# VectorE instead of GpSimd makes the low weight halves in the short convolution and first memory attention of a two-block float32 model

## The chip, the cores and the metric

The kernel runs as one program on one core of a Trainium2 chip. The core has a matrix engine (TensorE, PE in the rows), three engines for elementwise work (VectorE or DVE, ScalarE or ACT, GpSimd or POOL) and SyncE (SP), which here only issues loads. The metric is device time of one execution in microseconds, smaller being better.

## The reference, cut to what matters

The reference applies two blocks to 512 tokens of width 1024 in float32. The part that the change touches is the middle of the second block's first layer: a short gated convolution over 768 channels, and an attention of 512 queries over 256 memory tokens.

```
def short_conv_mixer(h, w_in, conv_w):
    proj = h @ w_in
    gate_b, gate_c, xt, q_mem = jnp.split(proj, [CONV_CH, 2 * CONV_CH, 3 * CONV_CH], axis=-1)
    y = gate_b * causal_short_conv(gate_c * xt, conv_w)
    return y, q_mem

def memory_attention(q_mem, mem, mem_norm_g, w_mem_kv, g_q, g_k):
    q = rms_norm(q_mem.reshape(b, s, MEM_HEADS, MEM_HEAD_DIM), g_q)
    k, v = jnp.split(rms_norm(mem, mem_norm_g) @ w_mem_kv, 2, axis=-1)
    k = rms_norm(k.reshape(b, m, MEM_HEADS, MEM_HEAD_DIM), g_k)
    ...
    p = jax.nn.softmax(scores, axis=-1).astype(v.dtype)
    o = jnp.einsum('bhqm,bmhd->bqhd', p, v)
...
        x = x + jnp.concatenate([y_mix, y_mem], axis=-1) @ w_out[layer]
```

## The kernel before, in words

Activations are kept transposed: channels on the 128 partitions, 512 tokens along the free dimension. Every weight matrix is cut into panels of 128x1024, each of which holds eight 128x128 blocks, and the panels are streamed from HBM in the order in which they are used (table `STAGES`, whose first number is the panels of a stage). One panel makes one 128x512 tile of output, in a bank of PSUM.

Each float32 product is made of three passes in a shorter type (fp32r). The weight panel is split into a high half `w_hi`, a rounded copy, and a low half `w_lo`, what the rounding left over; the activations have halves `h_hi` and `h_lo` likewise. A panel is then 8 x 3 matmuls: `w_hi*h_hi` (L640), `w_hi*h_lo` (L641) and `w_lo*h_hi` (L642).

A panel n passes four engines. SyncE loads it into one of four slots of `raw` once the low half of panel n-4 is made. ScalarE writes `w_hi` (L1259) into one of two slots, once TensorE has finished panel n-2. Then either VectorE (L1735) or GpSimd (L595) subtracts `w_hi` from `raw` into `w_lo`. TensorE waits for that low half, by one of the two counters `lo_ready` and `lo_by_pool`, and starts the panel.

Which engine makes the low half is read from the table `POOL_RUNS` (line 95): four runs of panel numbers belong to GpSimd, all others to VectorE. GpSimd has nothing else to do in a run but to wait for each `hi_ready` and subtract. VectorE's program is one fixed list of instructions written out by hand, in which a call `split(n)` stands at the place where panel n's low half is made, between the other work of the stage; `split` issues nothing for a panel of a GpSimd run. All engines work through their lists strictly in order.

The run named `conv` spans 23 panels, from the third panel of stage `conv0` to the first of `wo0`. The stages there are `conv0` (6 panels, two groups of three for the convolution), `qm0` (2, the queries of the memory attention), `conv1` (3), `mem0` (4, keys and values of 256 memory tokens, so that their matmuls are only 256 columns wide), `conv` (9, with the attention's steps between the panels) and `wo0` (8). I call the panels c0.0 to c0.5, q.0 and q.1, c1.0 to c1.2, m.0 to m.3, and c.0 to c.8.

VectorE's list there is, in short: for three panels of `conv0`, scale the tile by `rstd` (`scaled`, L1805), multiply, convolve (L1824, L1828), multiply, and make the halves of the result (L1740, L1741); then `memory_squares`, 16 instructions of 128x256 that sum the squares of the memory tokens; then the next three panels, the two of `qm0`, and `memory_input` for tiles 0 to 3 and, after the tile of c1.0, for tiles 4 to 7: three instructions of 128x256 each (L2370, L1740, L1741), which make the right-hand side of `mem0`. The lines that decide where a low half stands among these are:

```
                p = 3 * (j - head) + part
                if p or st is not ST["conv0"]:
                    split(st.n + p + 1)
...
            for j in range(4):
                split(ST["mem0"].n + j + 1)
```

Of the kernel before, what the change touches and what calls it, by code (L numbers as in the profile page):

```python
# [83 lines left out]
def schedule():  # L84
    out, n, t, s = {}, 0, 0, 0
    for name, panels, tiles, units in STAGES:
        out[name] = Stage(n, t, s, panels, tiles, units)
        n, t, s = n + panels, t + tiles, s + units
    return out, n


ST, PANELS = schedule()


POOL_RUNS = {"first": (ST["xbc"].n, ST["br0"].n),
             "conv": (ST["conv0"].n + 2, ST["wo0"].n), "s1a": (ST["s1a_in0"].n + 2, ST["s1a_in"].n - 1),
             "mla": (ST["mla_in"].n + 2, ST["wo1"].n)}


# [88 lines left out]
def at(c, i, step):  # L188

    return c if i is None else i * step + c  # L190
# [69 lines left out]
def build(nc, A, out):  # L260
    with ExitStack() as ctx:
# [292 lines left out]
        @block.sync  # L554
        def _(sp):
            wst = A["wstream"]
            sp.dma_start(vec[:, 0:DT], A["vec"][:, 0:DT]).then_inc(gain_loaded, 16)
            sp.dma_start(raw[:, 0], wst[0]).then_inc(w_loaded[0], 16)
            for k in range(DT):
                sp.dma_start(x[:, k], A["x"][:, k]).then_inc(x_loaded[k], 16)  # L560
            sp.dma_start(mats[:, 0:2], A["mats"][:, 0:2]).then_inc(ones_loaded, 16)
            sp.dma_start(raw[:, 1], wst[1]).then_inc(w_loaded[1], 16)
            sp.dma_start(mats[:, 2:], A["mats"][:, 2:]).then_inc(const_loaded, 16)
            sp.dma_start(vec[:, DT:], A["vec"][:, DT:]).then_inc(const_loaded, 16)
            for n in range(2, RAW):
                sp.dma_start(raw[:, n], wst[n]).then_inc(w_loaded[n], 16)

            def load(n, i=None):

                sp.wait_ge(lo_of(n), at(split_count(n), i, RAW))  # L570
                src = wst[n + RAW] if i is None else wst[bass.ds(i * RAW + (n + RAW), 1)].rearrange("a p n -> (a p) n")
                sp.dma_start(raw[:, n % RAW], src).then_inc(w_loaded[n % RAW], 16)

            for first, last in split_runs():
                last = min(last, PANELS - RAW - 1)
                rounds = (last - first + 1) // RAW
                if rounds > 1:
                    with sp.Fori(0, rounds) as i:
                        for n in range(first, first + RAW):
                            load(n, i)  # L580
                    first += rounds * RAW
                for n in range(first, last + 1):
                    load(n)


        @block.gpsimd
        def _(pool):
            def split_run(run):

                first, last = POOL_RUNS[run]  # L590
                whole = (last - first + 1) // RAW

                def one(n, i=None):
                    pool.wait_ge(hi_ready, at(n + 1, i, RAW))
                    nc.gpsimd.tensor_tensor(w_lo[:, n % HL], raw[:, n % RAW], w_hi[:, n % HL].bitcast(F32), ALU.subtract)\  # L595
                        .then_inc(lo_by_pool, 1)
                with pool.Fori(0, whole) as i:
                    for n in range(first, first + RAW):
                        one(n, i)
                for n in range(first + whole * RAW, last + 1):  # L600
                    one(n)

            split_run("first")
            pool.wait_ge(posted, ST["br0"].s + 8)
            pool.dma_start(rope_r[:], A["rope_r"]).then_inc(side_loaded, 16)
            pool.wait_ge(side_loaded, 16)
            pool.dma_start(tmp[:], A["ret_decay"]).then_inc(side_loaded, 16)
            pool.wait_ge(side_loaded, 32)
            for c in range(DT):
                pool.wait_ge(posted, ST["br2"].s + c + 1)  # L610
                k = c // 2 + RET_HEADS * (c % 2)
                pool.dma_start(x_in[:, k], A["x"][:, k]).then_inc(x_again[k], 16)
            pool.wait_ge(posted, ST["s0a_out"].s + 8)
            pool.dma_start(mem_x[:], A["mem"]).then_inc(side_loaded, 16)
            pool.wait_ge(side_loaded, 48)
            split_run("conv")
            split_run("s1a")
            pool.wait_ge(posted, ST["s1a_out"].s + 8)
            pool.dma_start(mem_x1[:], A["mem"]).then_inc(side_loaded, 16)
            pool.wait_ge(side_loaded, 64)  # L620
            pool.dma_start(rope2[:, 0].bitcast(I32), A["positions"].to_broadcast([P, S])).then_inc(side_loaded, 16)
            pool.wait_ge(side_loaded, 80)
            split_run("mla")
            last = ST["s1b_out"]
            for t in range(DT):
                pool.wait_ge(posted, last.s + t + 1)
                pool.dma_start(out[:, t], x[:, t]).then_inc(out_stored, 16)
            pool.wait_ge(out_stored, 16 * DT)
# [1091 lines left out]
        def _(dve):  # L1720
# [172 lines left out]
            def att_unit(a, u):  # L1893

                for first in range(a.ahead - 1) if u == 0 else ():
                    att_max(a, first)
                w = a.width(u)
                dve.wait_ge(a.exp_done, a.u0 + u + 1)
                done(v.reciprocal(small[:, a.columns(u, 2)], small[:, a.columns(u, 1)]))
                for e in range(a.chunks):  # L1900
                    prob = a.prob(u)[:, w * e:w * e + w]
                    ins = v.tensor_scalar(prob, prob, small[:, a.columns(u, 2, e)], None, ALU.mult)
                ins.then_inc(a.prob_ready, 1)
                if u + a.ahead - 1 < a.n:
                    att_max(a, u + a.ahead - 1)
                for hd in a.due(u, 1):
                    tile, _, last = a.tile(hd)
                    if last:
                        att_out(a, tile)
# [782 lines left out]
```

## Time and profile before

| | |
|---|---|
| time, median of 3 runs | 3110.13 us (3108.36 to 3115.47) |
| the profiled execution's own time | 3119.87 us |
| its span, first to last instruction | 3118.0 us |
| mean granted TensorE clock | 0.988 |
| TensorE busy | 3063.2 us, 98% |
| VectorE busy | 1822.0 us, 58% |
| ScalarE busy | 944.6 us, 30% |
| GpSimd busy | 247.1 us, 8% |

The span runs from the first to the last instruction, and the time of the execution is 1.87 us more. The stretch that the change concerns lies at about 1509 to 1680 us of the span. TensorE's clock is shown as a fraction of full speed; it has the two levels 2.4 and 1.2 GHz, so 0.50 is the lower one. In a timeline row the first number is the start in us, the second the duration in us, and the brackets at the end tell how long the engine had been idle and what released it.

### The profile page before, as it was taken

How to read it: one execution, taken by the hardware profiler on the slowest of the kernel's cores; microseconds unless marked ns; L12 is line 12 of the kernel's file. 1: busy time of each engine (PE TensorE's matmuls, PEld its weight loads, DVE VectorE, ACT ScalarE, POOL GpSimd, SP SyncE). 2: the span in 40 equal slices, each digit the busy share in tenths (PEclk: the TensorE clock that was granted, in tenths of full speed). 3: DMA queues.
4: the chain of work that ended last, by engine and by line, in shares of the span. 5: the costliest groups of instructions: out<-in, count | busy, mean ns of one | idle time of the engine just before them, and what ended most of it. 6: DMA issues, size and time to landing. Idle time of an engine off the chain costs nothing.

```text
span 3118.0 us, 36947 instructions
## 1 busy us (share of the span) xinstructions
PE 3063.2 (98%) x13711; PEld 2479.8 (80%) x13711; DVE 1822.0 (58%) x2429; ACT 944.6 (30%) x1294; POOL 247.1 (8%) x119
## 2 busy tenths in 40 slices
PE   8999999999999999999989999999999999999999
PEld 7787788787888878888777888887888886588887
DVE  8896565667666555554757554455554545565532
ACT  3644543333222222222222222222222243322222
POOL 0043330000000000000231000001000130000000
PEclk9999999999999999999999999999999997999999
DMA  4222133233223222223322223332233310023232
GB/s 143 95 94 81 62 101 115 68 108 102 94 95 100 96 92 92 98 94 108 108 81 75 95 94 101 102 101 88 97 98 103 110 62 27 22 96 98 94 108 88
DMA packets 79372, 287.60 MB, mean 92 GB/s; under 512 B 9056, under 2 KB 9312, under 8 KB 78880
## 3 DMA queue, kind: packets, MB, share of 16 engines
q1 hardware_dynamic: 77328, 277.96, 27.2%
q0 software_dynamic: 1936, 8.13, 0.8%
q8 instruction: 76, 1.25, 0.2%
q14 instruction: 32, 0.26, 0.0%
HBM read 283.96 MB, written 2.10 MB: 92 GB/s over the span
## 4 chain that ended last, share of the span: by engine, by line
PE 85%; issue 9%; DVE 3%; POOL 2%; ACT 1%; DMA 0%; POOLq 0%; DVEq 0%; ACTq 0%
PE ps L640 26%; PE ps L641 26%; PE ps L642 26%; POOL w_lo L595 2%; PE ps L733 1%; PE ps L1215 1%; PE ps L749 1%; PE ps L1076 1%; PE ps L1016 1%; PE ps L799 1%; PE ps L1221 1%; PE ps L1214 1%; PE ps L1082 0%; DVE w_lo L1735 0%; PE ps L698 0%
## 5 line engine op out<-in xcount | busy, mean ns | idle before, releaser
L1259 ACT ACTIVATE w_hi<-raw 128x1024 fp32r<-128x1024 f32 x525 | 555.5, 1058 | 1372.5 <-PE ps L642 1368.6
L640 PE MATMUL ps<-h_hi,w_hi 128*128 128x512 f32 (+1 forms) x2379 | 934.2, 393 | 6.8 <-DVE w_lo L1735 3.3
L641 PE MATMUL ps<-h_lo,w_hi 128*128 128x512 f32 (+1 forms) x2379 | 924.5, 389 | 0.0
L642 PE MATMUL ps<-h_hi,w_lo 128*128 128x512 f32 (+1 forms) x2379 | 924.2, 388 | 0.0
L1735 DVE TENSOR_TENSOR w_lo<-raw,w_hi 128x1024 fp32r<-128x1024 f32 x431 | 526.9, 1222 | 474.8 <-ACT w_hi L1259 469.8
L640 PEld LDWEIGHTS ps<-h_hi,w_hi 128*128 128x128 f32 x2379 | 448.2, 188 | 111.3 <-issue 11.2
L642 PEld LDWEIGHTS ps<-h_hi,w_lo 128*128 128x128 f32 x2379 | 447.9, 188 | 92.9
L641 PEld LDWEIGHTS ps<-h_lo,w_hi 128*128 128x128 f32 x2379 | 448.1, 188 | 92.1 <-issue 2.2
L640 PE MATMUL ps<-mid_hi,w_hi 128*128 128x512 f32 x1208 | 471.3, 390 | 2.2 <-DVE mid_lo L1810 2.1
L642 PE MATMUL ps<-mid_hi,w_lo 128*128 128x512 f32 x1208 | 470.7, 390 | 0.0
L641 PE MATMUL ps<-mid_lo,w_hi 128*128 128x512 f32 x1208 | 470.7, 390 | 0.0
L595 POOL TENSOR_TENSOR w_lo<-raw,w_hi 128x1024 fp32r<-128x1024 f32 x94 | 235.4, 2505 | 957.9 <-ACT w_hi L1259 949.9
L640 PEld LDWEIGHTS ps<-mid_hi,w_hi 128*128 128x128 f32 x1208 | 227.2, 188 | 51.1 <-DVE mid_lo L1810 3.5
L642 PEld LDWEIGHTS ps<-mid_hi,w_lo 128*128 128x128 f32 x1208 | 227.2, 188 | 47.4
L641 PEld LDWEIGHTS ps<-mid_lo,w_hi 128*128 128x128 f32 x1208 | 227.1, 188 | 47.2 <-issue 0.2
L1805 DVE TENSOR_TENSOR stage<-ps,rstd 128x512 f32<-128x512 f32 x104 | 71.8, 691 | 231.7 <-PE ps L642 231.6
L1264 ACT ACTIVATE stage<-ps 128x512 f32<-128x512 f32 x108 | 64.2, 599 | 372.3 <-PE ps L642 359.2
L640 PE MATMUL ps<-br_hi,w_hi 128*128 128x512 f32 x256 | 102.0, 398 | 11.2 <-DVE br_lo L1810 8.9
L1805 DVE TENSOR_TENSOR tmp<-ps,rstd 128x512 f32<-128x512 f32 x73 | 50.4, 691 | 99.8 <-PE ps L642 99.6
L642 PE MATMUL ps<-br_hi,w_lo 128*128 128x512 f32 x256 | 100.4, 392 | 0.0
L641 PE MATMUL ps<-br_lo,w_hi 128*128 128x512 f32 x256 | 100.4, 392 | 0.0
L1577 ACT ACTIVATE tmp<-tmp 128x512 f32<-128x512 f32 x112 | 69.3, 619 | 74.3 <-DVE tmp L1828 58.3
(402 smaller groups left out, 2616.8 us busy)
## 6 DMA issues: line engine op xcount, KB each, us to landing
raw<-in_wstream SPq DMA_DIRECT2D x525, 512.0 KB, 3.3
x<-in_x SPq DMA_DIRECT2D x8, 256.0 KB, 5.6
x_in<-in_x POOLq DMA_DIRECT2D x8, 256.0 KB, 3.1
mem_x<-in_mem POOLq DMA_DIRECT2D x2, 1024.0 KB, 5.1
out<-x POOLq DMA_DIRECT2D x8, 256.0 KB, 3.5
tmp<-in_ret_decay POOLq DMA_DIRECT2D x1, 1024.0 KB, 5.7
rope_r<-in_rope_r POOLq DMA_DIRECT2D x1, 512.0 KB, 4.0
mats<-in_mats SPq DMA_DIRECT2D x1, 256.0 KB, 6.5
```

What stands on the lines that cost most here:

```text
L595: nc.gpsimd.tensor_tensor(w_lo[:, n % HL], raw[:, n % RAW], w_hi[:, n % HL].bitcast(F32), ALU.subtract)\
L640: nc.tensor.matmul(dst, hi_w, hi_x, start=first, stop=False)
L641: nc.tensor.matmul(dst, hi_w, lo_x, start=False, stop=False)
L642: return nc.tensor.matmul(dst, lo_w, hi_x, start=False, stop=last)
L733: mm = nc.tensor.matmul(dst[:, n.heads * c:n.heads * c + n.heads], tmp[:, n.slots[j], P * c:P * c + P], ones, start=j == 0, stop=j == n.ti ...
L749: mm = nc.tensor.matmul(dst[rows, P * c:P * c + P], small[:, k:k + 1].to_broadcast([P, P // n.heads]), IDENT, start=True, stop=True)
L799: mm = nc.tensor.transpose(dst[:, o:o + P], a.prob(u)[:, w * e + P * c:w * e + P * c + P], IDENT)
L1259: nc.scalar.activation(w_hi[:, n % HL], raw[:, r], ACT.Copy).then_inc(hi_ready, 1)
L1264: nc.scalar.activation(dst, src[rows, 0:cols], func, bias=bias, scale=scale).then_inc(drained, 1)
L1577: nc.scalar.activation(tmp[:, s % 2], tmp[:, s % 2], func).then_inc(act_done, 1)
L1735: v.tensor_tensor(w_lo[:, n % HL], raw[:, n % RAW], w_hi[:, n % HL].bitcast(F32), ALU.subtract)\
L1805: v.tensor_tensor(dst, bank(t), scale, ALU.mult).then_inc(drained, 1)
```

## The change

The entry `conv` is taken out of `POOL_RUNS`, and the call that ran it out of GpSimd's program. The 23 panels then belong to VectorE by the same table, on all engines that ask it: `split` issues their low halves at the places where its calls already stand, TensorE and SyncE wait for `lo_ready` there, and GpSimd goes from its load of `mem_x` straight to waiting for the next run.

```
 POOL_RUNS = {"first": (ST["xbc"].n, ST["br0"].n),
-             "conv": (ST["conv0"].n + 2, ST["wo0"].n), "s1a": (ST["s1a_in0"].n + 2, ST["s1a_in"].n - 1),
+             "s1a": (ST["s1a_in0"].n + 2, ST["s1a_in"].n - 1),
              "mla": (ST["mla_in"].n + 2, ST["wo1"].n)}
...
             pool.dma_start(mem_x[:], A["mem"]).then_inc(side_loaded, 16)
             pool.wait_ge(side_loaded, 48)
-            split_run("conv")
             split_run("s1a")
```

The changed file has one line less, so VectorE's L1735 of before is L1734 of after, and so on.

First place: VectorE's list around `memory_squares`, between the third and the fourth panel of `conv0`. Before, from the end of the first convolution group:

```order
L1740 CAST cat_hi<-tmp 128x512
L1741 TENSOR_TENSOR cat_lo<-tmp,cat_hi 128x512
L1795 MEMSET acc 128x512
L1787 TENSOR_TENSOR stage<-mem_x 128x256
L1788 TENSOR_TENSOR acc<-acc,stage 128x256
...
L1805 TENSOR_TENSOR tmp<-ps,rstd 128x512
L1805 TENSOR_TENSOR stage<-ps,rstd 128x512
```

The same place in the changed program:

```order
L1739 CAST cat_hi<-tmp 128x512
L1740 TENSOR_TENSOR cat_lo<-tmp,cat_hi 128x512
L1794 MEMSET acc 128x512
L1786 TENSOR_TENSOR stage<-mem_x 128x256
L1787 TENSOR_TENSOR acc<-acc,stage 128x256
...
L1734 TENSOR_TENSOR w_lo<-raw,w_hi 128x1024
L1804 TENSOR_TENSOR tmp<-ps,rstd 128x512
L1734 TENSOR_TENSOR w_lo<-raw,w_hi 128x1024
L1804 TENSOR_TENSOR stage<-ps,rstd 128x512
```

The first `w_lo` is that of c0.4, the second that of c0.5. The one of c0.4 now stands behind the 17 instructions of `memory_squares`.

Second place: VectorE's list around `memory_input`, in stage `conv1`. Before, from the last of tiles 0 to 3 on:

```order
L1741 TENSOR_TENSOR mem_lo<-acc,mem_hi 128x256
L1805 TENSOR_TENSOR tmp<-ps,rstd 128x512
L2370 SCALAR_TENSOR_TENSOR acc<-mem_x,vec,spare 128x256
L1740 CAST mem_hi<-acc 128x256
...
L1741 TENSOR_TENSOR mem_lo<-acc,mem_hi 128x256
L1805 TENSOR_TENSOR stage<-ps,rstd 128x512
L2398 TENSOR_TENSOR cpad<-tmp,stage 128x512
```

The same place in the changed program:

```order
L1740 TENSOR_TENSOR mem_lo<-acc,mem_hi 128x256
L1734 TENSOR_TENSOR w_lo<-raw,w_hi 128x1024
L1804 TENSOR_TENSOR tmp<-ps,rstd 128x512
L2369 SCALAR_TENSOR_TENSOR acc<-mem_x,vec,spare 128x256
L1739 CAST mem_hi<-acc 128x256
...
L1740 TENSOR_TENSOR mem_lo<-acc,mem_hi 128x256
L1734 TENSOR_TENSOR w_lo<-raw,w_hi 128x1024
L1804 TENSOR_TENSOR stage<-ps,rstd 128x512
L2397 TENSOR_TENSOR cpad<-tmp,stage 128x512
```

The two `w_lo` are those of c1.1 and c1.2; each stands behind twelve instructions of `memory_input`.

Third place: VectorE's list at stage `mem0`. Before, from the end of the third convolution group:

```order
L1740 CAST cat_hi<-tmp 128x512
L1741 TENSOR_TENSOR cat_lo<-tmp,cat_hi 128x512
L1860 TENSOR_TENSOR tmp<-mem_k 128x256 x2
L1805 TENSOR_TENSOR tmp<-ps,rstd 128x512
L1868 RECIPROCAL small<-small 128x4 x2
```

The same place in the changed program:

```order
L1739 CAST cat_hi<-tmp 128x512
L1740 TENSOR_TENSOR cat_lo<-tmp,cat_hi 128x512
L1734 TENSOR_TENSOR w_lo<-raw,w_hi 128x1024 x4
L1859 TENSOR_TENSOR tmp<-mem_k 128x256 x2
L1734 TENSOR_TENSOR w_lo<-raw,w_hi 128x1024
L1804 TENSOR_TENSOR tmp<-ps,rstd 128x512
```

The four are the low halves of m.1, m.2, m.3 and c.0, one behind the other, and the single one is that of c.1.

## Rows read from the trace of the kernel before

**Rows 1.** The page: engines, and the two costliest groups that make low halves

```profile
PE 3063.2 (98%) x13711; PEld 2479.8 (80%) x13711; DVE 1822.0 (58%) x2429; ACT 944.6 (30%) x1294; POOL 247.1 (8%) x119
...
L1735 DVE TENSOR_TENSOR w_lo<-raw,w_hi 128x1024 fp32r<-128x1024 f32 x431 | 526.9, 1222 | 474.8 <-ACT w_hi L1259 469.8
...
L595 POOL TENSOR_TENSOR w_lo<-raw,w_hi 128x1024 fp32r<-128x1024 f32 x94 | 235.4, 2505 | 957.9 <-ACT w_hi L1259 949.9
```

**Rows 2.** Timeline of TensorE: starts of c0.2, c0.3, m.0 to m.3, c.0

```profile
1523.03 0.50 PE L640 MATMUL ps<-h_hi,w_hi 128*128 128x512 f32 x1
...
1528.60 0.39 PE L640 MATMUL ps<-h_hi,w_hi 128*128 128x512 f32 x1
...
1572.61 0.28 PE L640 MATMUL ps<-mem_hi,w_hi 128*128 128x256 f32 x1
...
1576.44 0.38 PE L640 MATMUL ps<-mem_hi,w_hi 128*128 128x256 f32 x1 [0.80 <-POOL w_lo L595]
...
1583.93 0.58 PE L640 MATMUL ps<-mem_hi,w_hi 128*128 128x256 f32 x1 [4.35 <-POOL w_lo L595]
...
1589.83 0.28 PE L640 MATMUL ps<-mem_hi,w_hi 128*128 128x256 f32 x1
...
1593.29 0.50 PE L640 MATMUL ps<-h_hi,w_hi 128*128 128x512 f32 x1 [0.80 <-POOL w_lo L595]
```

**Rows 3.** Windows of 4 us: length, PE busy (count), granted clock, DMA, GB/s

```profile
1580.00:1584.00 4.00, 0.07 (x1) 0.87 0.00 0
1584.00:1588.00 4.00, 4.00 (x19) 0.50 0.52 151
```

**Rows 4.** Timeline of TensorE in a later stage, around a shorter stall

```profile
2130.97 0.50 PE L640 MATMUL ps<-mid_hi,w_hi 128*128 128x512 f32 x1 [1.88 <-DVE mid_lo L1810]
...
2133.33 0.63 PE L640 MATMUL ps<-mid_hi,w_hi 128*128 128x512 f32 x1
...
2135.89 0.42 PE L640 MATMUL ps<-mid_hi,w_hi 128*128 128x512 f32 x1
```

**Rows 5.** Timeline of ScalarE: high halves after c0.3, q.1, c1.0; the drain of m.0

```profile
1534.30 1.06 ACT L1259 ACTIVATE w_hi<-raw 128x1024 fp32r<-128x1024 f32 x1 [4.38 <-PE ps L642]
...
1556.07 1.06 ACT L1259 ACTIVATE w_hi<-raw 128x1024 fp32r<-128x1024 f32 x1 [4.38 <-PE ps L642]
...
1561.99 1.06 ACT L1259 ACTIVATE w_hi<-raw 128x1024 fp32r<-128x1024 f32 x1 [4.50 <-PE ps L642]
...
1579.79 0.38 ACT L1264 ACTIVATE mem_k<-ps 128x256 f32<-128x256 f32 x1 [5.86 <-DVE stage L1805]
```

**Rows 6.** Timeline of GpSimd: the low half of c0.4

```profile
1530.00 2.54 POOL L595 TENSOR_TENSOR w_lo<-raw,w_hi 128x1024 fp32r<-128x1024 f32 x1 [3.40 <-ACT w_hi L1259]
```

**Rows 7.** Timeline of VectorE: first convolution group and the squares of the memory

```profile
1521.55 0.69 DVE L1805 TENSOR_TENSOR tmp<-ps,rstd 128x512 f32<-128x512 f32 x1
...
1528.87 0.69 DVE L1805 TENSOR_TENSOR stage<-ps,rstd 128x512 f32<-128x512 f32 x1 [0.42 <-PE ps L642]
...
1530.32 2.50 DVE L1740 CAST cat_hi<-tmp 128x512 fp32r<-128x512 f32 x1
...
1533.61 0.48 DVE L1795 MEMSET acc<- 128x512 f32 x1
...
1538.15 0.42 DVE L1787 TENSOR_TENSOR stage<-mem_x 128x256 f32<-128x256 f32 x1
...
1540.91 2.65 DVE L1787 TENSOR_TENSOR stage<-mem_x 128x256 f32<-128x256 f32 x1
```

**Rows 8.** Timeline of VectorE: the memory's reciprocal root and tiles 0 to 3

```profile
1557.52 1.75 DVE L2363 RECIPROCAL spare<-spare 128x256 f32<-128x256 f32 x1 [0.42 <-ACT spare L1319]
1559.31 0.58 DVE L2370 SCALAR_TENSOR_TENSOR acc<-mem_x,vec,spare 128x256 f32<-128x256 f32 x1
...
1562.97 0.48 DVE L2370 SCALAR_TENSOR_TENSOR acc<-mem_x,vec,spare 128x256 f32<-128x256 f32 x1
```

**Rows 9.** Timeline of VectorE in stage conv: one scaling

```profile
1635.18 0.69 DVE L1805 TENSOR_TENSOR stage<-ps,rstd 128x512 f32<-128x512 f32 x1 [4.47 <-PE ps L642]
```

More of the change, by code:

```diff
@@ L95 @@
 POOL_RUNS = {"first": (ST["xbc"].n, ST["br0"].n),
-             "conv": (ST["conv0"].n + 2, ST["wo0"].n), "s1a": (ST["s1a_in0"].n + 2, ST["s1a_in"].n - 1),
+             "s1a": (ST["s1a_in0"].n + 2, ST["s1a_in"].n - 1),
              "mla": (ST["mla_in"].n + 2, ST["wo1"].n)}
@@ L615, in _ @@
             pool.wait_ge(side_loaded, 48)
-            split_run("conv")
             split_run("s1a")
```

## The prediction

> **What bounds the kernel now.** I read the page first: TensorE is busy 98% of the span, VectorE 58%, GpSimd 8% [rows 1]. So the end is set by TensorE's panels and by the few places where TensorE waits, and a change that only reassigns elementwise work is worth what it adds to or takes from those waits. The same rows give the price of one low half: 1.22 us on VectorE (mean of 431), 2.5 us on GpSimd (mean of 94).
>
> Next I read TensorE's timeline through the stretch of the change. A panel of 512 columns takes 5.44 us: ScalarE's wait of 4.38 us plus its own 1.06 us repeat once a panel [rows 5]. One that follows a wait takes some 0.1 us more, as c0.2 does from 1523.03 to 1528.60 [rows 2]. TensorE loses nothing from there to m.0. Then it waits three times for GpSimd's low halves: 0.80 us before m.1, 4.35 us before m.2, 0.80 us before c.0 [rows 2]. The 4.35 us is followed by a stretch at a granted clock of 0.50, the 1.2 GHz level [rows 3], and m.2 takes 1589.83 - 1583.93 = 5.90 us [rows 2], against 8 x 3 matmuls in about 2.9 us for m.0 (3.83 us to the next start, less 0.80 idle and the slow restart).
>
> Last I asked why m.2 was late. ScalarE waited 5.86 us for VectorE's scaling of c1.2's tile before it could drain m.0 [rows 5]: that panel had ended at 1572.61, where m.0 starts, and VectorE came to it at 1579.06, the row's 1579.79 less 0.7 us for one scaling. VectorE was thus 6 us behind here. Until then its lateness had hurt nobody, since the low halves did not pass through it. That is the point of the argument: after the change they do.
>
> **A cost that goes.** In the rows of VectorE some instructions are 2 us too long: the cast at 1530.32 takes 2.50 us and ends with GpSimd's subtraction of 1530.00 to 1532.54 [rows 6, 7]; one square of 128x256 takes 2.65 us where its neighbour takes 0.42 [rows 7]. So nearly each of GpSimd's subtractions holds VectorE up for about 2.1 us. The Trainium skill (SBUF — State Buffer, Who interferes with whom) says that the two engines share a pair of ports under an exclusive lock, and that the second to come is blocked until the first ends; the trace agrees, with 2.50 us against 0.43. By that rule alone the move would shorten VectorE's work by about 2.1 - 1.2 = 0.9 us a panel, which speaks for a gain; it is the last of the rivals. I take the 2.1 us off wherever the trace shows one, from the rows and not from the rule.
>
> **The change, step by step.** I call the end of a panel 0.26 us before ScalarE's next high half (1534.30 for c0.3, whose end is then 1528.60 + 5.44 = 1534.04) [rows 2, 5].
>
> *A, c0.2.* GpSimd gave its low half for a start at 1523.03. VectorE now makes it behind the scaling of 1521.55 to 1522.24 [rows 7]: done at 1523.4, so +0.44 us.
>
> *B, c0.4.* c0.3 now ends at 1534.04 + 0.44 = 1534.5. VectorE goes on from the scaling of c0.2, 1528.87 + 0.44 = 1529.3. From there to the memset it took 4.74 us before, of which 2.07 was the held-up cast (2.50 against 0.43), so 2.67 us: the memset starts at 1532.0. Then 0.52 us for it, and 16 instructions at 0.46 (1538.15 to 1540.91 are six of them) [rows 7], 7.36 us: the low half starts at 1539.9, takes 1.22, and c0.4 starts at 1541.15. TensorE waits **+6.65 us** where it waited 0. Nothing hides it; behind it all of VectorE's and TensorE's list moves too. c0.5, q.0, q.1 and c1.0 do not wait again: VectorE has at most 5 us of work a panel there, of 5.44.
>
> *C, the clock behind B.* The nearest row is the 4.35 us wait, after which m.2 took 5.90 instead of about 3.0 us: **+2.9 us** [rows 2]. Bounds: 1.7 us (the shorter stall, below) and 3.4 us, twice that.
>
> *D, c1.1.* After the end of q.1 (1555.81), VectorE's reciprocal starts 1.71 us later, at 1557.52, and the first tile of `memory_input` 1.79 us after that; four tiles take 4.8 us (three took 3.66), then the low half 1.2: 9.5 us [rows 5, 8]. TensorE is done with c1.0 after 1561.99 - 1556.07 = 5.92 us [rows 5]. Stall **+3.6 us**.
>
> *E and F, the clock behind D, and c1.2.* In a later stage a wait of 1.88 us is followed by matmuls of 0.63 instead of 0.39 us, six of them in 2.56 us from 2133.33 to 2135.89, and nine or so in all: 1.7 us lost [rows 4]. I expect the same behind D. c1.2's low half stands behind a scaling, four tiles and itself, 0.66 + 4.8 + 1.2 = 6.65 us after that of c1.1, against a panel of 5.54: a wait of 1.1 us, which a slow c1.1 swallows. Together the larger: **+1.7 us** (bounds 1.1 and 2.9).
>
> *G, mem0.* From m.0's start to c.0's it took 1593.29 - 1572.61 = 20.7 us [rows 2]. Now VectorE is level with TensorE at the end of c1.2: 0.27 us to the scaling, 2.67 through the halves, 1.2 for the low half of m.1, so m.1 starts at 4.15 instead of at 2.9, a wait of 1.2. m.2 follows without one; m.3's high half comes 0.27 + 0.3 + 1.06 us after m.1's end at 7.0, its low half at 9.85, just when m.2 ends at 9.9; c.0 starts at 12.8. **-7.9 us**, from three waits made one and from 2.9 us of slow clock gone. Bounds: -8.8 if m.1 does not wait, -6 if m.2 and m.3 wait 1 us each.
>
> *The rest.* In `conv` the low half stands ahead of each scaling, that is before the panel's end that VectorE waits for anyway; in the attention units there it adds 1.2 us and the 2.1 us hold-ups go. 0, with bounds of -1 and +2. Loads start up to 6 us later behind B, and have three panels of slack: 0.
>
> Sum: 0.44 + 6.65 + 2.9 + 3.6 + 1.7 - 7.9 = **+7.4 us**. Against the profiled execution, 3118.0 us of span and 3119.87 us in all, that is 3125.4 and 3127.3; its time lies 9.7 us above the median of the runs, and I put the sum onto the median: 3110.1 + 7.4 = **3117.5 us**, +0.24%.
>
> **The rivals.** *Milder clock.* The stalls are as worked out, but the lower clock behind them is shorter or absent: B's at 1.7 and none behind D gives 0.44 + 6.65 + 1.7 + 3.6 + 1.1 - 7.9 = +5.6; no lower clock at all +3.9, so 3114 to 3115.7 us. For it: not every wait is followed by it (0.80 us before m.1 was not). Against: both stalls here are longer than the 1.88 us that was.
>
> *Later waits.* In the attention part VectorE is the engine that TensorE waits for, and a low half that queues behind a wait for ScalarE's exponentials or for a tile makes c.3 to c.8 late. At 1 to 2 us in three or four of six panels this gives +11 to +15, 3121 to 3125 us. Against: VectorE still has gaps there, 4.47 us before one of its scalings [rows 9].
>
> *The hold-ups were the real cost: faster.* If `memory_squares` and `memory_input` no longer delay a panel, because without GpSimd VectorE comes to them early enough, B to F vanish and -7.9 + 0.44 = -7.5 us is left, 3102.6 us. It decides at one point: VectorE would have to be at c0.4's low half by 1533.3, where I find 1539.9, and its 16 squares alone take 7.4 us of that stretch. I give it little.
>
> *No change in effect.* That B and G cancel: the backlog of VectorE is 6 us either way, and only its place moves, +2 to -2 us. For it: stalls of 0.44 + 6.65 + 3.6 + 1.1 + 1.2 against 5.95 before leave a difference that depends on the clock for half its size.
>
> **How the numbers follow.** My forecast, both stalls with a lower clock behind them (+5.8 to +9.5), 0.52; milder clock (+3.5 to +5.8) 0.23; later waits 0.10; no effect 0.09; faster 0.06. About 6.2 us, 0.2%, is what a measurement of this kernel can tell from no change, and it cuts my forecast's own range: 0.44 of its 0.52 lies above. So slower by over 0.2% is 0.44 + 0.10 = 0.54, within 0.2% 0.08 + 0.23 + 0.09 + 0.01 = 0.41, faster 0.05. The range goes from 3111.5, which leaves out the faster case and part of no effect, to 3122.5, which takes in the beginning of the later waits.
>
> **What would show it.** TensorE's waits in the new trace should name VectorE's low half: one of 6 to 7 us at about 1541, one of 3 to 4 us some 35 us later, one of about 1 us in `mem0`, and none for GpSimd in this stretch. Granted clock should be 0.50 just behind the first two and full in `mem0`. VectorE should show no cast or square over 1 us there. The prediction is wrong if c0.4 starts within 2 us of c0.3's end, if the waits come in `conv`, or if the slow stretch in `mem0` stays although its long wait is gone.

## The result, and the profile after

The changed kernel takes 3118.35 us (median of 20 runs, 3115.14 to 3126.64), the kernel before 3114.27 us (20 runs beside them, 3108.36 to 3118.77). The medians lie 4.1 us apart. The ratio of the two is given as 1.0019, with a 95% interval of 1.0013 to 1.0026, which is 5.9 us (4.0 to 8.1) slower. Forecast were 3117.5 us and +7.4 us.

The profiled execution of after took 3117.13 us, with a span of 3115.3 us. That is less than the 3118.0 us of the profiled execution before, although the medians go the other way. So two spans can't tell here what the change costs, and the stretch that it touches has to be cut out of the trace. I measure from VectorE's reciprocal at the head of `conv0` to its first low half in `wo0`. VectorE in the trace before, and in the trace after, where three of its rows in between stand too (start, duration, engine and line, operation, tiles, shapes):

```profile
1518.16 3.35 DVE L1799 RECIPROCAL rstd<-rstd 128x512 f32<-128x512 f32 x1 [1.94 <-ACT rstd L1299]
...
1678.93 1.23 DVE L1735 TENSOR_TENSOR w_lo<-raw,w_hi 128x1024 fp32r<-128x1024 f32 x1
```

```profile
1518.31 3.35 DVE L1798 RECIPROCAL rstd<-rstd 128x512 f32<-128x512 f32 x1 [1.94 <-ACT rstd L1298]
...
1530.84 0.43 DVE L1739 CAST cat_hi<-tmp 128x512 fp32r<-128x512 f32 x1
...
1539.91 1.23 DVE L1734 TENSOR_TENSOR w_lo<-raw,w_hi 128x1024 fp32r<-128x1024 f32 x1
...
1573.35 1.22 DVE L1734 TENSOR_TENSOR w_lo<-raw,w_hi 128x1024 fp32r<-128x1024 f32 x1
...
1684.94 1.23 DVE L1734 TENSOR_TENSOR w_lo<-raw,w_hi 128x1024 fp32r<-128x1024 f32 x1
```

The stretch is 1678.93 - 1518.16 = 160.77 us before and 1684.94 - 1518.31 = 166.63 us after: +5.86 us, which is what the ratio says (0.0019 x 3114.27 = 5.9). The rest of the span is 2957.2 us before and 2948.7 us after. Much of that difference arises in a later place that the change does not touch, and shows there in the granted clock (the number behind POOL's count). Two windows of 80 us from about the same point of the program, before and then after:

```profile
2465.00:2545.00 80.00, 76.87 (x385) 64.02 (x384) 36.31 (x55) 28.98 (x55) 23.17 (x11) 0.91 0.25 83
```

```profile
2471.00:2551.00 80.00, 76.99 (x419) 64.75 (x417) 40.62 (x59) 31.81 (x59) 25.20 (x12) 0.98 0.25 79
```

The stage was granted 0.91 in one execution, which started 385 matmuls in these 80 us, and 0.98 in the other, which started 419. One kernel alone varies as much from execution to execution: the 20 times of after go from 3115.14 us at a mean granted clock of 0.992 to 3126.64 us at 0.988. Over the kernels below the span outside the stretch goes from 2948.7 to 2959.7 us, and I take these 11 us for the same chance; that is inferred, since the one kernel that was profiled twice (after, and e8) repeated there within 0.7 us. It is more than the change itself.

The page of after, the lines that answer to [rows 1]:

```profile
PE 3054.4 (98%) x13711; PEld 2471.8 (79%) x13711; DVE 1816.4 (58%) x2452; ACT 944.8 (30%) x1294; POOL 189.9 (6%) x96
...
L1734 DVE TENSOR_TENSOR w_lo<-raw,w_hi 128x1024 fp32r<-128x1024 f32 x454 | 554.9, 1222 | 481.6 <-ACT w_hi L1258 475.9
...
L595 POOL TENSOR_TENSOR w_lo<-raw,w_hi 128x1024 fp32r<-128x1024 f32 x71 | 178.2, 2510 | 1016.1 <-ACT w_hi L1258 1012.9
```

23 low halves have changed engine (431 to 454, 94 to 71). VectorE's busy time is nevertheless 5.6 us shorter, since 23 x 1.22 = 28 us of new work is less than the hold-ups by GpSimd that went. (Within the stretch it falls from 114.5 to 109.1 us, so these were worth 33.5 us, 1.5 us for each of the 23 subtractions.) By the sum of busy time the change is thus a saving. What it costs is in when the work comes, which TensorE's waits of this stretch (total, times, longest) and its timeline show:

```profile
PE ps L639 <- DVE w_lo L1734: 12.0, 5, 6.4
```

```profile
1523.57 0.50 PE L639 MATMUL ps<-h_hi,w_hi 128*128 128x512 f32 x1 [0.54 <-DVE w_lo L1734]
...
1541.19 0.80 PE L639 MATMUL ps<-h_hi,w_hi 128*128 128x512 f32 x1 [6.40 <-DVE w_lo L1734]
...
1543.92 0.63 PE L639 MATMUL ps<-h_hi,w_hi 128*128 128x512 f32 x1
...
1546.04 0.40 PE L639 MATMUL ps<-h_hi,w_hi 128*128 128x512 f32 x1
...
1574.62 0.50 PE L639 MATMUL ps<-h_hi,w_hi 128*128 128x512 f32 x1 [3.43 <-DVE w_lo L1734]
...
1581.08 0.50 PE L639 MATMUL ps<-h_hi,w_hi 128*128 128x512 f32 x1 [0.69 <-DVE w_lo L1734]
...
1586.66 0.28 PE L639 MATMUL ps<-mem_hi,w_hi 128*128 128x256 f32 x1
...
1590.66 0.39 PE L639 MATMUL ps<-mem_hi,w_hi 128*128 128x256 f32 x1 [0.96 <-DVE w_lo L1734]
...
1599.44 0.40 PE L639 MATMUL ps<-h_hi,w_hi 128*128 128x512 f32 x1
```

Where GpSimd was waited for three times, 6.0 us in all, VectorE is now waited for five times, 12.0 us in all, in front of c0.2, c0.4, c1.1, c1.2 and m.1. Windows behind the three longest waits, and ScalarE, whose high half of a panel starts 0.26 us behind the end of an earlier one:

```profile
1540.00:1544.00 4.00, 2.81 (x7) 2.23 (x8) 2.87 (x3) 0.00 (x0) 0.00 (x0) 0.50 0.37 125
...
1572.00:1576.00 4.00, 1.38 (x6) 1.14 (x7) 3.86 (x9) 0.34 (x1) 0.00 (x0) 1.00 0.07 16
1588.00:1592.00 4.00, 3.04 (x26) 2.83 (x25) 3.38 (x5) 1.33 (x2) 0.00 (x0) 1.00 0.22 70
```

```profile
1534.89 1.06 ACT L1258 ACTIVATE w_hi<-raw 128x1024 fp32r<-128x1024 f32 x1 [4.38 <-PE ps L641]
...
1549.04 1.06 ACT L1258 ACTIVATE w_hi<-raw 128x1024 fp32r<-128x1024 f32 x1 [13.10 <-PE ps L641]
...
1571.29 1.06 ACT L1258 ACTIVATE w_hi<-raw 128x1024 fp32r<-128x1024 f32 x1 [4.50 <-PE ps L641]
```

Behind the 6.4 us wait the clock is 0.50, the 1.2 GHz level, and the matmuls take 0.63 us until about 1545; behind the 3.43 us wait it is 1.00, the 2.4 GHz level, against my forecast; in `mem0` it is full where [rows 3] had 0.50.

### The profile page after: what moved, and what is told of

It is laid out like the page before. It is cut to its first block, busy times and chain, and to the rows that moved or that the text cites. A ratio compares the mean times of both kernels' runs of the same rounds, so it can differ in the third digit from the quotient of the medians.

```text
span 3115.3 us, 36928 instructions
## 1 busy us (share of the span) xinstructions
PE 3054.4 (98%) x13711; PEld 2471.8 (79%) x13711; DVE 1816.4 (58%) x2452; ACT 944.8 (30%) x1294; POOL 189.9 (6%) x96
## 4 chain that ended last, share of the span: by engine, by line
PE 86%; issue 8%; DVE 4%; POOL 1%; ACT 1%; POOLq 0%; ACTq 0%; DVEq 0%
PE ps L639 26%; PE ps L641 26%; PE ps L640 26%; POOL w_lo L595 1%; PE ps L732 1%; PE ps L1075 1%; PE ps L1214 1%; PE ps L748 1%; PE ps L1015 1%; DVE w_lo L1734 1%; PE ps L798 1%; PE ps L1220 0%; PE ps L1213 0%; PE ps L1081 0%; PE ps L697 0%
## 5 line engine op out<-in xcount | busy, mean ns | idle before, releaser
L1734 DVE TENSOR_TENSOR w_lo<-raw,w_hi 128x1024 fp32r<-128x1024 f32 x454 | 554.9, 1222 | 481.6 <-ACT w_hi L1258 475.9
L595 POOL TENSOR_TENSOR w_lo<-raw,w_hi 128x1024 fp32r<-128x1024 f32 x71 | 178.2, 2510 | 1016.1 <-ACT w_hi L1258 1012.9
```

The source lines that it names most:

```text
L1734: v.tensor_tensor(w_lo[:, n % HL], raw[:, n % RAW], w_hi[:, n % HL].bitcast(F32), ALU.subtract)\
```

## The experiments

All runs in one table, to be read with the texts below. "Waits" are TensorE's for low halves in the stretch. "Outside" is the span less the stretch. The first four were timed beside 35 runs of the kernel before (median 3112.95 us), the next four beside 27 (3112.99 us).

| kernel | waits us | stretch us | against before | outside us | median us (n) | ratio to before, 95% |
|---|---|---|---|---|---|---|
| before | 6.0 | 160.77 | | 2957.2 | 3114.27 (20) | |
| after | 12.0 | 166.63 | +5.86 | 2948.7 | 3118.35 (20) | 1.0019 (1.0013 to 1.0026) |
| e1, c0.4's half early | 7.7 | 161.28 | +0.51 | 2949.3 | 3113.92 (12) | 0.9999 (0.9991 to 1.0008) |
| e2, VectorE in front only | 11.9 | 169.05 | +8.28 | 2953.0 | 3122.18 (11) | 1.0018 (1.0010 to 1.0027) |
| e3, GpSimd in front only | 4.1 | 157.25 | -3.52 | 2951.1 | 3110.33 (12) | 0.9985 (0.9977 to 0.9994) |
| e4, filler in c0.4's wait | 6.2 | 166.36 | +5.59 | 2959.7 | 3119.39 (12) | 1.0015 (1.0005 to 1.0025) |
| e5, squares on ScalarE | 5.8 | 160.72 | -0.05 | 2956.1 | 3118.57 (11) | 1.0009 (0.9999 to 1.0020) |
| e6, rebalanced | 1.2 | 152.83 | -7.94 | 2949.2 | 3104.99 (11) | 0.9977 (0.9968 to 0.9986) |
| e7, GpSimd busy beside | 15.1 | 172.40 | +11.63 | 2950.3 | 3124.45 (5) | 1.0042 (1.0028 to 1.0056) |
| e8, after once more | 11.3 | 167.06 | +6.29 | 2949.4 | 3118.10 (11) | 1.0022 (1.0011 to 1.0033) |

### e1: is the place of one low half the whole cost?

To after, with c0.4's low half put ahead of the 16 squares:

```diff
-                if p or st is not ST["conv0"]:
+                if st is not ST["conv0"] or p not in (0, 3):
                     split(st.n + p + 1)
...
             for part in range(3):
                 conv_part(st, 0, part, 0)
+            split(st.n + 4)
             memory_squares(48, mem_x, 5)
```

> The changed kernel, with c0.4's low half moved ahead of memory_squares on VectorE; nothing else differs. I measure by the stretch from VectorE's reciprocal of rstd before conv0 to its first low half in wo0: 160.8 us in the trace of before, 166.6 in that of after. Theory (VectorE is behind by all its work, the place of one low half only chooses who pays): the 6.4 us wait at c0.4 goes, but c0.5's low half now comes some 2.9 us late, and c1.1 and c1.2 wait as in the changed kernel (3.4 and 0.8). Stretch 160 to 162 us, time -4.5 to -6 us against the changed kernel. Rival (one badly placed low half is the whole cost): the 6.4 us and the 2.0 us of lower clock behind them go and nothing comes back, stretch 158 us or less, no wait at c0.5.

TensorE's timeline of e1, and a window behind its longest wait:

```profile
1543.12 0.50 PE L639 MATMUL ps<-h_hi,w_hi 128*128 128x512 f32 x1 [2.70 <-DVE w_lo L1734]
...
1569.11 0.50 PE L639 MATMUL ps<-h_hi,w_hi 128*128 128x512 f32 x1 [3.43 <-DVE w_lo L1734]
```

```profile
1569.00:1575.00 6.00, 5.89 (x19) 4.69 (x20) 5.73 (x15) 0.00 (x0) 0.00 (x0) 0.72 0.26 87
```

c0.4 no longer waits. But c0.5 does, 2.70 us where it did not before, since the squares now lie in front of its low half. 7.7 us of waits stay, the time returns to that of before and no further. From the reciprocal to the start of m.0 it takes 54.45 us before, 68.35 in after and 63.20 in e1: of the 13.9 us that the steps A to F cost (below), 5.2 are gone and the rest has stayed. So the queue of work on VectorE sets the price, and one badly placed half is not the whole of it.

### e2 and e3: which half of the change costs, which gives?

e2 leaves `mem0` from m.1 on, and `conv`, to GpSimd. e3 is its reverse: GpSimd from c0.2 to m.1 and VectorE from m.2 on. `split_run("conv")` stands again in GpSimd's list in both, over these runs of panels:

```diff
# e2
+             "conv": (ST["mem0"].n + 1, ST["wo0"].n),
# e3
+             "conv": (ST["conv0"].n + 2, ST["mem0"].n + 1),
```

> Half of the change: VectorE makes the low halves of c0.2 to m.0, GpSimd again those of m.1 to the first of wo0. Theory: this half holds all of the cost and little of the gain, since VectorE's lateness is already spent in waits at c0.4, c1.1 and c1.2 when mem0 begins; in mem0 GpSimd's 2.5 us per panel gives waits of about 1, 0.4, 1 and 0.4 us. Stretch 168 us (166 to 169.5), time +6 to +8 us against before. Rival (GpSimd's slowness made mem0 slow before): the 4.35 us wait before m.2 comes back with its lower clock, stretch 172 us or more.

> The other half: GpSimd makes c0.2 to m.1 as before, VectorE m.2 to the first of wo0. Theory: no wait at c0.4, c1.1 or c1.2; before m.1 0.8 to 1 us as before; before m.2 3 to 4 us, because ScalarE and VectorE are late there by VectorE's lateness and not by GpSimd; no wait before c.0. Stretch 155.5 to 159 us (the higher value with a lower clock behind the wait before m.2), time -2 to -5 us against before and -6 to -10 against the changed kernel. Rival (VectorE, already behind, is made later still by four low halves in a row): m.2 or m.3 wait over 5 us and the stretch is 161 us or more.

TensorE's waits in e2 and its starts of m.0 and c.0 there, then its timeline in e3 (the last row is c.0) with a window behind the second wait:

```profile
PE ps L640 <- DVE w_lo L1735: 10.4, 3, 6.4
PE ps L640 <- POOL w_lo L595: 1.5, 2, 0.9
```

```profile
1588.43 0.28 PE L640 MATMUL ps<-mem_hi,w_hi 128*128 128x256 f32 x1
...
1602.64 0.50 PE L640 MATMUL ps<-h_hi,w_hi 128*128 128x512 f32 x1
```

```profile
1578.57 0.39 PE L640 MATMUL ps<-mem_hi,w_hi 128*128 128x256 f32 x1 [0.80 <-POOL w_lo L595]
...
1584.99 0.58 PE L640 MATMUL ps<-mem_hi,w_hi 128*128 128x256 f32 x1 [3.28 <-DVE w_lo L1735]
...
1592.18 0.47 PE L640 MATMUL ps<-h_hi,w_hi 128*128 128x512 f32 x1
```

```profile
1584.00:1590.00 6.00, 5.01 (x30) 5.01 (x31) 2.07 (x2) 0.96 (x3) 0.00 (x0) 0.72 0.52 175
```

The front part alone costs more than the whole change, by the stretch: e2's is 8.28 us longer than before. (By the ratios of the times, 1.0018 against 1.0019, the two can't be told apart.) The part behind m.1 alone is a gain: 3.52 us in e3, whose time is below that of before by its whole interval. But the two don't add up to after (8.28 - 3.52 = 4.8 against 5.86 to 6.29). The gap itself is no larger than what the clock can do: behind c.0 e2 is 1.0 us longer than after, with a granted clock of 0.63 over 8 us where after had 0.79. The overlap of the two halves shows in `mem0`. From m.0 to c.0 it takes 20.7 us before [rows 2], 1592.18 - 1574.73 = 17.4 in e3 (its m.0 starts at 1574.73), 1602.64 - 1588.43 = 14.2 in e2 and 12.8 in after. There the halves give 6.5 + 3.2 = 9.7 us, and the whole change 7.9. So 6.5 of the 7.9 us of my term G come in e2 as well, where GpSimd makes these halves as before. They come because TensorE has waited in front and VectorE is level when `mem0` begins. Only the last 1.4 us come from faster halves. The 4.35 us wait of [rows 2] was in the same way three quarters VectorE's lateness: in e3, where VectorE itself makes that half in 1.2 us, m.2 still waits 3.28.

### e4: is the loss behind c0.4's wait the clock?

To after, six products of a constant matrix in front of c0.4, into a bank that is free there, which the kernel does not use:

```diff
             for j in range(6):
+                for _ in range(6 if j == 4 else 0):
+                    nc.tensor.matmul(ps[:, 7], ONES, mats[:, 0:4].rearrange("p a n -> p (a n)"), start=True, stop=True)
                 conv_part(ST["conv0"], j, new_x("s0a_out") if j == 0 else None)
```

> The changed kernel, with six float32 matmuls of constants into an unused PSUM bank put into TensorE's list ahead of c0.4, where it waits 6.4 us for VectorE; they take about 5.2 us in all and their result is not used. Theory (the 2.0 us by which c0.4 is longer than a panel are the lower granted clock, which falls because TensorE idles): granted clock stays 1.00 from 1536 to 1548, c0.4 takes 5.5 instead of 7.5 us, stretch 164.6 us, time -2 us and less spread from run to run. Rival (c0.4 is slow for another reason, such as its low half or a queue): c0.4 still takes 7.5 us and the stretch is 166.6 or more.

```profile
1536.32 5.31 PE L1094 MATMUL ps<-mats 128*128 128x512 f32 x12
1542.89 0.50 PE L639 MATMUL ps<-h_hi,w_hi 128*128 128x512 f32 x1 [1.26 <-DVE w_lo L1736]
...
1574.36 0.80 PE L639 MATMUL ps<-h_hi,w_hi 128*128 128x512 f32 x1 [3.44 <-DVE w_lo L1736]
```

```profile
1542.00:1548.00 6.00, 5.11 (x22) 4.22 (x23) 2.57 (x3) 0.00 (x0) 0.00 (x0) 1.00 0.55 177
...
1574.00:1580.00 6.00, 5.64 (x13) 4.46 (x14) 5.73 (x15) 0.00 (x0) 0.00 (x0) 0.50 0.27 87
```

That is e4's TensorE, timeline and windows; the first row counts two instructions for each of the six products. c0.4 starts as late as in the changed kernel (1542.89 here, against 1542.72 in e8, both with VectorE's reciprocal at about 1520), but at 0.50 instead of 0.80 us for its first matmul and at a granted clock of 1.00 instead of 0.62, and it takes 5.6 us instead of 7.4 (e8) or 7.6 (after). So the second part of c0.4's delay is the clock, and the clock followed the idle time and not the lateness. The other half of the expectation failed: the stretch is no shorter, because the 3.44 us wait at c1.1, which after's first profile had without a loss, was here followed by a clock of 0.50. Nor were the times lower or closer together: they go from 3115.45 to 3127.87 us.

### e5: is it the length of VectorE's list?

To after, the squares of the memory on ScalarE, and three additions on VectorE in place of the memset and 16 instructions:

```diff
...
+                if n == ST["conv0"].n + 2:
+                    act.wait_ge(side_loaded, 48)
+                    for k in range(DT):
+                        nc.scalar.activation(probs[:, k // 2, MEM * (k % 2):MEM * (k % 2) + MEM], mem_x[:, k], ACT.Square)\
+                            .then_inc(mem_squared, 1)
...
             def memory_squares(loaded, mem, summed):
-                clear_acc()
-                dve.wait_ge(side_loaded, loaded)
-                for k in range(DT):
-                    square_sum(mem[:, k], acc_ready if k == DT - 1 else None, MEM, stage[:, 0])
+                dve.wait_ge(mem_squared, DT)
+                done(v.tensor_tensor(probs[:, 0:2], probs[:, 0:2], probs[:, 2:4], ALU.add))
+                done(v.tensor_tensor(probs[:, 0], probs[:, 0], probs[:, 1], ALU.add))
+                v.tensor_tensor(acc[:, 0:MEM], probs[:, 0, 0:MEM], probs[:, 0, MEM:], ALU.add).then_inc(acc_ready, 1)
```

> The changed kernel, with the squares of the memory tokens made by ScalarE (8 activations of 128x256 behind its high half of c0.3, into the unused buffer of the attention's probabilities), so that VectorE's memory_squares is three additions instead of a memset and 16 instructions; about 2.4 us instead of 7.9. The same result is computed. Theory (the wait at c0.4 is the length of the block that its low half stands behind): the wait falls from 6.4 to 1.0 us (0.7 to 1.4), the lower clock behind it is gone, the waits at c1.1 and c1.2 stay at 3.4 and 0.8. Stretch 158.5 to 160.5 us, time -6 to -8 us against the changed kernel. Rival (VectorE's total work sets the pace, so that a shorter block only moves the wait on): the wait shows up again at c0.5 or q.0, or c1.1's grows by more than 1 us, and the stretch is 162 us or more.

```profile
1534.02 0.50 PE L639 MATMUL ps<-h_hi,w_hi 128*128 128x512 f32 x1 [0.84 <-DVE w_lo L1739]
...
1565.45 0.80 PE L639 MATMUL ps<-h_hi,w_hi 128*128 128x512 f32 x1 [3.43 <-DVE w_lo L1739]
```

```profile
1565.00:1571.00 6.00, 5.55 (x13) 4.40 (x14) 5.72 (x15) 0.00 (x0) 0.00 (x0) 0.50 0.25 87
```

With 2.4 us of VectorE's work there instead of 7.9, the wait at c0.4 goes from 6.40 to 0.84 us: the block of squares was that wait, us for us. At c1.1 nothing changes, 3.43 us, as its block is another one (the reciprocal and four tiles). The clock behind it was 0.50 in this execution, and the stretch came out 0.2 us above what I had given. The expected gain of 6 to 8 us shows in the stretch and not in the time: e5's median is 3118.57 us, that of e8, the changed kernel timed beside it, 3118.10. By the ratios e5 is 4 us faster (1.0009 against 1.0022), with intervals that overlap. Of its eleven times six lie at 3118.6 to 3120.9 us and five at 3109.3 to 3115.0. Why they part I did not find.

### e6: a version that beats both?

From before, GpSimd keeps its halves up to m.2's. The squares are as in e5. The sum of squares and its root stand one panel earlier, so that the memory's tiles are made during q.1 and c1.0. ScalarE makes m.2's high half before it drains m.0:

```diff
-             "conv": (ST["conv0"].n + 2, ST["wo0"].n),
+             "conv": (ST["conv0"].n + 2, ST["mem0"].n + 2),
...
-            memory_sum(5)
+                if j == 0:
+                    memory_sum(5)
...
-                if n == ST["conv1"].n:
+                if n == ST["qm0"].n + 1:
                     memory_root(spare[:, 0])
...
+                    elif j < 3:
+                        split(st.n + j + 2)
...
-            memory_rms(r)
-            memory_input(0, mem_x, r, mem_hi, mem_lo, range(0, 4))
+                if j == 0:
+                    memory_rms(r)
+                memory_input(0, mem_x, r, mem_hi, mem_lo, range(2 * j, 2 * j + 2))
```

> A version meant to beat both: from the kernel before, GpSimd makes the low halves up to m.2 and VectorE from m.3 on; the squares are made by ScalarE as in the run beside this; the sum of squares is taken after q.0 instead of q.1, so that memory_input starts a panel earlier; and ScalarE makes m.2's high half before it drains m.0. The same result is computed. Theory (before lost 6 us and 3 us of clock in mem0 because VectorE came to it 6 us late, and the changed kernel pays the same lateness earlier): with 6 us less of VectorE's work ahead of it mem0 has one wait of about 0.8 us at m.1 and none over 1 us after it. Stretch 151.5 to 154 us, time -6 to -9 us against before. Rival (GpSimd's 2.5 us per panel of 2.9 us, behind ScalarE's 1.1, is the bound in mem0): waits before m.2 and m.3 of 2 us or more, stretch 156 us or more.

```profile
PE ps L640 <- POOL w_lo L595: 1.2, 2, 0.9
```

Of the waits for low halves 1.2 us are left (e6's waits of TensorE), none for VectorE. The stretch is 152.83 us, 7.94 us under before and 13.8 us under after. At 3104.99 us (3101.87 to 3107.75) it is the fastest kernel of this study. It changes four things at once, and no run tells what each of them is worth.

### e7: do GpSimd's instructions hold VectorE up?

To after, one subtraction of constants on GpSimd for each panel from c0.2 to c1.2, into a buffer that is not in use there, so that no other engine waits for its data:

```diff
+            for n in range(ST["conv0"].n + 2, ST["mem0"].n):
+                pool.wait_ge(hi_ready, n + 1)
+                nc.gpsimd.tensor_tensor(ckv[:].rearrange("p a n -> p (a n)")[:, 0:6 * P], mats[:].rearrange("p a n -> p (a n)"),
+                                        mats[:].rearrange("p a n -> p (a n)"), ALU.subtract).then_inc(extra, 1)
+                pool.wait_ge(extra, n - ST["conv0"].n - 1)
```

> The changed kernel, with GpSimd subtracting constants (128x768, float32, some 1.9 us) into an unused buffer at each high half of the nine panels c0.2 to c1.2; nothing uses the result. It puts back only what GpSimd's work costs VectorE. Theory (a subtraction of GpSimd holds VectorE's instructions with two operands in SBUF up for its whole length): single casts and squares of 1.7 to 2.3 us appear, the waits at c0.4 and c1.1 grow by 2.5 to 4 and 1.4 to 3 us, stretch 171 to 174 us, time +3.5 to +7 us against the changed kernel. Rival (the long casts of before were something else, for instance loads landing): no VectorE instruction of this stretch grows beyond its usual length by over 0.5 us, stretch 166.6 +- 1 us.

GpSimd and VectorE in e7, in the order of time, and TensorE's waits:

```profile
1532.45 1.48 POOL L619 TENSOR_TENSOR ckv<-mats 128x768 f32<-128x768 f32 x1 [4.44 <-ACT w_hi L1264]
...
1538.23 1.47 POOL L619 TENSOR_TENSOR ckv<-mats 128x768 f32<-128x768 f32 x1 [4.30 <-ACT w_hi L1264]
```

```profile
1532.63 1.57 DVE L1745 CAST cat_hi<-tmp 128x512 fp32r<-128x512 f32 x1
...
1538.26 1.72 DVE L1792 TENSOR_TENSOR stage<-mem_x 128x256 f32<-128x256 f32 x1
```

```profile
PE ps L645 <- DVE w_lo L1740: 15.1, 5, 8.5
```

The cast takes 1.57 us instead of 0.43, the square 1.72 instead of 0.42, and each ends when or just after GpSimd does (1532.45 + 1.48 = 1533.93 against 1534.20; 1539.70 against 1539.98). The delay reaches TensorE: the wait at c0.4 is 8.49 instead of 6.40 us and the stretch 172.40 instead of 166.63. The sizes were expected larger: GpSimd's instruction takes 1.48 us and not 1.9, the two of VectorE are below or at the edge of the 1.7 to 2.3 us given, and the waits grow by 2.1 us at c0.4 and 1.2 at c1.1 (4.58 us), under the ranges of 2.5 to 4 and 1.4 to 3. The rule of the Trainium skill that the prediction weighed (SBUF — State Buffer, Who interferes with whom) agrees with these rows.

### e8: the change once more, beside the others

The kernel after, unchanged.

> The changed kernel once more, unaltered, so that it is timed on the same chip as the three others and its clock is seen in a second execution. Theory (the lower clock behind a wait of 3.4 us comes in some executions and not in others, which moves single times by 2 to 3 us here and as much in later stages): the waits at c0.4, c1.1 and c1.2 are again 6.4, 3.4 and 0.8 us to 0.1, the stretch is 166 to 168.5, and what lies outside it differs from the first profile's 2948.7 us by up to 9 us. Rival (the clock is the same each time, and the kernels differ elsewhere for a reason in them): stretch and remainder repeat within 0.5 us.

```profile
1542.72 0.79 PE L639 MATMUL ps<-h_hi,w_hi 128*128 128x512 f32 x1 [6.39 <-DVE w_lo L1734]
...
1575.94 0.50 PE L639 MATMUL ps<-h_hi,w_hi 128*128 128x512 f32 x1 [3.43 <-DVE w_lo L1734]
```

```profile
1542.00:1548.00 6.00, 5.28 (x15) 4.24 (x16) 2.40 (x3) 0.00 (x0) 0.00 (x0) 0.62 0.55 173
...
1576.00:1582.00 6.00, 6.00 (x19) 4.75 (x20) 5.73 (x14) 0.00 (x0) 0.00 (x0) 0.72 0.24 87
```

e8's timeline and windows. The waits at c0.4 and c1.1 are the same to 0.01 us as in the first profile of after. The clock behind the second one is 0.72 instead of 1.00, c1.1 is 1.6 us longer for it (10.8 instead of 9.2 us between the ends of c1.0 and c1.1 that ScalarE's rows give), and c1.2, whose low half is ready meanwhile, does not wait. This is steps E and F as I had put them. The expectation had a wait of 0.8 us at c1.2 and missed that. The span outside the stretch repeated within 0.7 us, so the difference of up to 9 us that was thought possible there did not show between these two.

## Why the prediction was right

Each step by the starts and ends of panels in the first profile of after. The ends are ScalarE's rows less 0.26 us, and 0.15 us is taken off where a time of after is set against one of before, since its reciprocal starts that much later.

| step | forecast | measured in after | from |
|---|---|---|---|
| A, c0.2 | +0.44 | +0.44 | end of c0.3: 1534.89 against 1534.30, less 0.15 |
| B, c0.4 starts late | +6.65 | +6.56 | 1541.19 - 1534.63 |
| C, clock behind B | +2.9 | +2.15 | c0.4 ends at 1548.78, 7.59 us after its start, less 5.44 |
| D, c1.1 starts late | +3.6 | +3.59 | 1574.62 - 1571.03 |
| E and F | +1.7 | +1.16 | what is left to the start of m.0: 1586.66 - 1572.61 - 0.15 = 13.90 in all |
| G, mem0 | -7.9 | -7.9 | m.0 to c.0: 1599.44 - 1586.66 = 12.78 against 20.68 |
| the rest | 0 | -0.14 | 5.86 less the above |
| sum | +7.4 | +5.86 | |

*The backlog* (B, D, G) came where it was put and within 0.1 us. c0.4's low half starts at 1539.91 on VectorE, where 1539.9 had been worked out from rows of the kernel before. e1 shows that the squares in front of it are what it waits for, since without them it is in time; e5 that it is their length; e2 and e3 that the cost lies in front of m.1, and that most of G is that same lateness, paid earlier.

*The lower clock* (C, E) was mis-sized, and this makes 1.3 of the 1.5 us that the sum is too high. C was taken as 2.9 us from m.2's slow stretch, and that was misread. The start of m.3 was put at 1589.83, but m.2's 24 matmuls from 1583.93 end before that, and m.3 starts at 1589.21, still at the lower clock. TensorE's timeline of before:

```profile
1589.00 0.41 PE L642 MATMUL ps<-mem_hi,w_lo 128*128 128x256 f32 x1
1589.21 0.41 PE L640 MATMUL ps<-mem_hi,w_hi 128*128 128x256 f32 x1
```

m.2 took 5.28 us, not 5.90, and m.3 the other slow matmuls; together they took 2.6 us more than two panels of 2.88. So 2.6 was what these rows had to give for C. c0.4, with its longer wait, lost 2.15 us, 1.9 in e8 and 1.6 in e2. That it is the clock is shown by e4. For E I had taken for settled that a lower clock follows, since it follows a wait of 1.88 us in [rows 4]. In the first profile it did not, in e8 it did, and E and F together were then 1.8 us, forecast as 1.7. So the step that was too firm is the sentence "I expect the same behind D": it is a matter of the single execution, and worth 0.6 us between these two, and 1.7 us between after and e4 or e5, where E and F together were 2.9.

*The hold-ups* were real (e7), and the cast is back at 0.43 us in after. That nearly each subtraction costs VectorE 2.1 us was too much: beside the 23 of them only 14 instructions of VectorE were over 0.5 us too long, and the mean cost was 1.5 us. They did not decide: VectorE had time for them where nothing of TensorE's passed through it. *The milder clock*, the nearest rival, describes the first profile's c1.1 and leaves c0.4 in the middle (2.15 us, between its 1.7 and my 2.9). Its +5.6 us is nearer to the two measured stretches, +5.86 and +6.29, than my +7.4; these lie at the lower end of my case's own range. The waits are those of both cases, and the clock behind them is that of the one in one execution and of the other in the next. *Later waits* did not come: the rest is -0.14 us. *No change in effect*, at +2 to -2 us, and *faster* are outside the interval. Taken alone, though, the move behind m.1 is faster, as e3 shows, and the first half of *no change* is right: of the backlog that `mem0` paid for, 6.5 us were only paid elsewhere.

*Luck in the number.* That 3117.5 us lies within 0.9 us of the measured 3118.35 is in part luck. The base was the median of three runs, 3110.1 us, and 20 runs gave 3114.3, 4.1 us more; the effect was smaller than +7.4, by 1.5 us in the stretch and 3.3 in the medians. The two errors cancel. And 0.54 was put on a slowdown of over 0.2%, while 0.19% was measured, with an interval on both sides of that line: which of the two it is stays undecided.

Still open: whether the lower clock follows a wait of 3.4 us can't be told from the wait, see below. And the span outside the stretch differs by up to 11 us between profiled executions, so an effect of this size shows in medians of many runs or in the cut-out stretch, and not in one span.

## What to carry to other kernels

When work comes back to an in-order engine, ask for each piece what stands ahead of it in that engine's list and whether TensorE waits for it: the 23 halves made VectorE's busy time shorter and the kernel slower, since two of them stood behind blocks of 7.9 and 6.5 us. Move it where the engine is level and leave it where it has a block to work off (e3), shorten or spread the block (e5; e6, with other changes, gave 7.9 us of a stretch of 161), and don't credit a change with a wait that goes further down only because the engine's lateness has been paid for earlier (6.5 of the 7.9 us in `mem0`). Compare such variants over the stretch that they touch, between two instructions that none of them moves, because the rest of the span carries its own chances.

## What the runs showed of the hardware

The same wait of TensorE of 3.43 or 3.44 us, in front of the same panel c1.1, was followed by three different clocks. From the end of c1.0 to the end of c1.1 it took 9.2 us in after at a granted clock of 1.00, 10.8 in e8, e1 and e2 at 0.72 over the 6 us behind it, and 11.9 in e4 and e5 at 0.50; the wait and a panel at full clock make 8.9 of them. Kernel and wait do not decide it, as after and e8 are one program. The cost of such a wait beyond itself was thus 0.3, 1.9 or 3.0 us. The 6.4 us wait cost 2.15 us in after, 1.9 in e8 and 1.6 in e2; in e7 a wait of 4.58 us cost 1.5 and one of 8.49 us 2.1. The longer wait is not the one with the largest extra. The Trainium skill (TensorE: Matmul & The Clock Gate, Part 1: The HAM clock gate) says that the chip's monitor of TensorE's activity runs freely and is not started by the kernel, so that one kernel shows different slow stretches from run to run; after and e8 agree with that, and no run here shows what the monitor looks at.
